# A two-block float32 transformer on one core: seven stretches of work put in another order, and the narrow level products done in 32x32 blocks

## What is computed

```python
def first_block(x, ...):
    hn = rms_norm(h, mix_norm_pre)
    rq, rk, rv, rg, aq, ak, av, iq, ik, iw = split_columns(hn @ w_in)
    ret_out = retention(rope(rq), rope(rk), rv, rg)
    att_out = dsa_attention(rope(aq), rope(ak), av, rope(iq), rope(ik), iw)
    mixed = concatenate([ret_out, att_out]) @ w_out
    h = h + rms_norm(mixed, mix_norm_post)          # post(0)
    ffn = conv_ffn(rms_norm(h, ffn_norm_pre))
    h = h + rms_norm(ffn, ffn_norm_post)            # post(1)

def hgrn2_mixer(h, ...):       # one gated linear attention, 8 heads of 128
    q, f, i, g = split(h @ w_in)
    log_f = log_sigmoid(f); k = -expm1(log_f)
    # causal: o_t = sum_s<=t (q_t * exp(G_t - G_s) . k_s) v_s, G the running sum of log_f
    o = rms_norm(o, out_norm) * silu(g)
    return o @ w_out                                # "mix2"

def nsa_mixer(h, ...):
    # keys and values of 31 compressed blocks of 32 tokens:
    kc = rms_norm(silu((k_cmp + pos) @ w1) @ w2); vc = silu((v_cmp + pos) @ w1) @ w2
    # attention over compressed keys, over all allowed keys, over a window
    return (g0 * o_cmp + g1 * o_sel + g2 * o_win) @ w_out
```

## Time and profile before

| | us |
|---|---|
| median of 3 runs | 2195.03 |
| lowest, highest | 2194.46, 2196.22 |
| profiled execution, its own time | 2194.65 |
| its span | 2192.9 |
| TensorE busy | 2090.3 (95% of the span) |
| VectorE busy | 1260.3 |
| ScalarE busy | 797.7 |
| GpSimd busy | 79.6 |

### The profile page before, as it was taken

The page is one execution under the profiler, slowest core; times in us unless marked ns, Lnnn a source line. Parts: engine busy times, 40 slices in busy tenths (PEclk is TensorE's granted clock), DMA queues, the critical chain, the costliest instruction groups (busy, mean ns, idle before and its releaser), DMA issues.

```text
span 2192.9 us, 28478 instructions
## 1 busy us (share of the span) xinstructions
PE 2090.3 (95%) x10920; PEld 1706.6 (78%) x10920; DVE 1260.3 (57%) x2218; ACT 797.7 (36%) x1444; POOL 79.6 (4%) x79
## 2 busy tenths in 40 slices
PE   6999889999998999989999999999789999999998
PEld 5778568888886878887888888779756677888887
DVE  3577747787744447654555555676676747322334
ACT  3323543333424551243322232433446634222222
POOL 0012000000000001000000000001001100000000
PEclk9999889999999999999999999999899999999999
DMA  5221025565532221102556445322300013433221
GB/s 194 88 94 39 13 75 173 176 196 168 168 128 86 87 96 59 58 20 87 173 173 201 165 163 183 125 68 90 118 1 2 2 59 123 128 98 99 100 96 48
DMA packets 146690, 231.34 MB, mean 105 GB/s; under 512 B 7324, under 2 KB 83708, under 8 KB 146556
## 3 DMA queue, kind: packets, MB, share of 16 engines
q1 hardware_dynamic: 144300, 224.05, 31.4%
q0 software_dynamic: 864, 3.15, 0.4%
q10 hardware_dynamic: 1392, 2.33, 0.3%
HBM read 227.41 MB, written 2.10 MB: 105 GB/s over the span
## 4 chain that ended last, share of the span: by engine, by line
PE 83%; DVE 9%; ACT 4%; issue 3%; DMA 0%; POOL 0%; DVEq 0%; POOLq 0%; SPq 0%; ACTq 0%
PE ps L2253 11%; PE ps L2255 11%; PE ps L2254 11%; PE ps L2280 4%; PE ps L2483 4%; PE ps L2282 4%; PE ps L2281 4%; PE ps L2211 4%; PE ps L2212 4%; PE ps L2213 4%; PE ps L2551 4%; PE ps L2481 3%; PE ps L2301 2%; PE ps L2313 2%; PE ps L2326 2%
## 5 line engine op out<-in xcount | busy, mean ns | idle before, releaser
L1557 DVE TENSOR_TENSOR w_lo<-ring,w_hi 128x1024 fp32r<-128x1024 f32 (+4 forms) x362 | 378.9, 1048 | 740.5 <-ACT w_hi L977 740.1
L977 ACT ACTIVATE w_hi<-ring 128x1024 fp32r<-128x1024 f32 (+4 forms) x362 | 329.5, 912 | 1013.0 <-PE ps L2255 469.9
L2253 PE MATMUL ps<-x_hi,w_hi 128*128 128x512 f32 x1056 | 416.2, 394 | 0.0
L2255 PE MATMUL ps<-x_hi,w_lo 128*128 128x512 f32 x1056 | 411.2, 389 | 0.0
L2254 PE MATMUL ps<-x_lo,w_hi 128*128 128x512 f32 x1056 | 410.9, 389 | 0.0
L2254 PEld LDWEIGHTS ps<-x_lo,w_hi 128*128 128x128 f32 x1056 | 198.5, 188 | 42.6 <-issue 1.9
L2253 PEld LDWEIGHTS ps<-x_hi,w_hi 128*128 128x128 f32 x1056 | 198.5, 188 | 42.4 <-issue 1.9
L2255 PEld LDWEIGHTS ps<-x_hi,w_lo 128*128 128x128 f32 x1056 | 198.3, 188 | 41.6
L2280 PE MATMUL ps<-w_hi,x_hi 128*128 128x512 f32 x480 | 187.5, 391 | 4.0 <-DVE x_hi L1633 4.0
L2282 PE MATMUL ps<-w_hi,x_hi 128*128 128x512 f32 x480 | 186.8, 389 | 0.0
L2281 PE MATMUL ps<-w_lo,x_hi 128*128 128x512 f32 x480 | 186.8, 389 | 0.0
(11 more groups left out here) (343 smaller groups left out, 3069.2 us busy)
## 6 DMA issues: line engine op xcount, KB each, us to landing
ring<-in_ada_w SPq DMA_DIRECT2D x48, 1024.0 KB, 5.1
ring<-in_ffn_w_in SPq DMA_DIRECT2D x88, 512.0 KB, 4.7
ring<-in_w_up SPq DMA_DIRECT2D x44, 512.0 KB, 4.7
ring<-in_ffn_w_out SPq DMA_DIRECT2D x20, 1024.0 KB, 4.9
ring<-in_hgrn_w_in SPq DMA_DIRECT2D x16, 1024.0 KB, 5.2
ring<-in_w_in SPq DMA_DIRECT2D x12, 1024.0 KB, 5.1
ring<-in_w_down SPq DMA_DIRECT2D x10, 1024.0 KB, 4.9
ring<-in_kv_ada_w SPq DMA_DIRECT2D x8, 1024.0 KB, 5.1
```

The source lines that it names most:

```text
L977: a.activation(to[:, n % depth, 0:src.shape[-1]], src, ACT.Copy).then_inc(s["hi_done"], 1)
L1557: v.tensor_tensor(to[:, n % depth, 0:width], src, hi[:, n % depth, 0:width].bitcast(F32), ALU.subtract).then_inc(s["lo_done"], 1)
L2253: mm(bs[j], wh[:, k, c], x_hi[:, 2 * q + k], start=first, stop=False)
L2255: ins = mm(bs[j], wl[:, k, c], x_hi[:, 2 * q + k], start=False, stop=last)
```

## The change

It has nine edits.

1. The banks of the first projection unit are shifted by one: row tile t is written to bank (t + 1) % 4, its turned form too.
2. In the DSA attention, TensorE turns the first four column tiles of mix1 (`turn_half`) ahead of the last four transposes of the attention's output, and ScalarE splits the first weight piece of mix1 after the last copy of the attention.
3. In `post(0)` ScalarE squares y of all token tiles before it squares the new x of the tiles 1 to 3, and VectorE does y_weighted and y_added of each tile together, x_normed of tile 0 after tile 1, and the other x_normed after all y_added.
4. In `post(1)` the same, with `ada_columns(0)` ahead of two x_normed in place of one.
5. The level products for the levels -1 to 4 multiply 16 blocks of 32 x 32 on the diagonal for each of the two heads, in place of 4 blocks of 128 x 128.
6. In mix2 ScalarE and VectorE split the first weight piece one loop step earlier, and TensorE multiplies the first two pieces before the turn of the last head.
7. VectorE's `split_q` (the split of x for the queries) begins at the fourth piece of the key/value projection, not at the first.
8. In PREP the fourth part of the first compression product comes before query chunk 2, the second product before chunk 3, the turn of the keys after chunk 4; VectorE's `cmp_sums`, `cmp_keys` and `cmp_turned` come one chunk earlier, ScalarE's root too.
9. In the NSA attention, the same as 2 for mix3.

```diff
--- before.py
+++ after.py
@@ -392,12 +392,12 @@
             for t in range(NT):
-                plan_bank((name, t), 4 * (k % 2) + t)
+                plan_bank((name, t), 4 * (k % 2) + ((t + 1) % NT if k == 0 else t))
             if k == 0:
...
                 for t in range(NT):
-                    plan_bank((P1_ORDER[k - 1], "T", t), 4 * ((k - 1) % 2) + t)
+                    plan_bank((P1_ORDER[k - 1], "T", t), 4 * ((k - 1) % 2) + ((t + 1) % NT if k == 1 else t))
             if k == INDEX_UNIT:
@@ -479,8 +479,8 @@
-        PREP = [("cmp1", 0, 0), ("q", 0), ("cmp1", 0, 1), ("q", 1), ("cmp1", 1, 0), ("q", 2), ("cmp1", 1, 1), ("q", 3), ("cmp2",),
-                ("q", 4), ("q", 5), ("cmpT",), ("q", 6), ("q", 7)]
+        PREP = [("cmp1", 0, 0), ("q", 0), ("cmp1", 0, 1), ("q", 1), ("cmp1", 1, 0), ("cmp1", 1, 1), ("q", 2), ("cmp2",), ("q", 3),
+                ("q", 4), ("cmpT",), ("q", 5), ("q", 6), ("q", 7)]
         for t in range(NT):
@@ -907,11 +907,12 @@
                             y_square(stage, t, half)
-                        if t:
-                            x_rms(i, t - 1)
+                        if t == 1:
+                            x_rms(i, 0)
+                    for t in range(1, NT):
+                        x_rms(i, t)
                     if i not in (2, 4):
                         early_highs(i, slice(0, 1))
-                    x_rms(i, NT - 1)
                 else:
@@ -983,6 +984,8 @@
                     else:
+                        if (n, i) == (0, 0):
+                            filled(act, ("dsa", "B", NT - 1))
                         out_weight(name, i)
@@ -1225,9 +1228,9 @@
                     a.activation(x_hi[:, i - 3], p, ACT.Copy).then_inc(s["out_hi"], 1)
-                if i > HH:
-                    out_weight("mix2", i - HH - 1)
-            for i in range(2, 8):
+                if i >= HH:
+                    out_weight("mix2", i - HH)
+            for i in range(3, 8):
                 out_weight("mix2", i)
...
@@ -1402,15 +1405,14 @@
                         y_weighted(stage, half, t)
-                    if t >= 1:
-                        y_added(stage, t - 1)
-                    if t >= 2:
-                        x_normed(i, t - 2)
-                y_added(stage, NT - 1)
-                x_normed(i, NT - 2)
+                    y_added(stage, t)
+                    if t == 1:
+                        x_normed(i, 0)
+                x_normed(i, 1)
                 if stage == 1:
                     ada_columns(0)
-                x_normed(i, NT - 1)
+                for t in range(2, NT):
+                    x_normed(i, t)
                 if i != 2:
...
@@ -2017,8 +2019,8 @@
                 low((key, k), n_piece(w, key, k), w2_lo, w2_hi)
-                if g < KT:
-                    split_q(g)
+                if 3 <= g < KT + 3:
+                    split_q(g - 3)
                 if g >= N_LAG:
@@ -2093,11 +2095,11 @@
                 q_chunk(i)
+                if i == 3:
+                    cmp_sums()
                 if i == 4:
-                    cmp_sums()
+                    cmp_keys()
                 if i == 5:
-                    cmp_keys()
-                if i == 6:
                     cmp_turned()
@@ -2291,7 +2293,7 @@
-            def attention(name, ready):
+            def attention(name, turn_half):
                 unit_of, n_units, (L, PB, PT, OT), base = ATT[name]
@@ -2329,6 +2331,8 @@
                         g = (j - 7) // 4
+                        if g == n_units // 8 - 1:
+                            turn_half()
                         b = open_bank((name, "B", g))
@@ -2337,22 +2341,26 @@
                 wait()
-                for kt in range(KT):
+                for kt in range(4, KT):
                     turn(lambda t: src[:, t, kt * P:(kt + 1) * P], (name, "T", kt))
...
-            def piece_gemm(name):
+            def gemm_piece(name, u, q, bs):
+                if u == 0:
+                    for kt in (2 * q, 2 * q + 1):
+                        evacuated(pe, (name, "T", kt))
+                split_piece((name, u), q, [(name, u, t) for t in range(NT)], bs, 512)
+            def piece_gemm(name, done=0, bs=None):
...
                 for u in range(2):
-                    bs = [None] * NT
-                    keys = [(name, u, t) for t in range(NT)]
-                    for q in range(4 if u == 0 else 2):
-                        if u == 0:
-                            for kt in (2 * q, 2 * q + 1):
-                                evacuated(pe, (name, "T", kt))
-                        split_piece((name, u), q, keys, bs, 512)
+                    if u or not done:
+                        bs = [None] * NT
+                    for q in range(0 if u else done, 2 if u else 4):
+                        gemm_piece(name, u, q, bs)
                     if u == 1:
-                        split_piece((name, u), None, keys, bs, 512, order=LAST_ORDER)
+                        split_piece((name, u), None, [(name, u, t) for t in range(NT)], bs, 512, order=LAST_ORDER)
@@ -2424,10 +2432,15 @@
                         ins.then_inc(full(("ret_o", t)), 1)
-            attention("dsa", None)
+            def turn_ret():
+                pe.wait_ge(s["mixed_ready"], NT)
+                for kt in range(4):
+                    turn(lambda t: mixed[:, t, kt * P:(kt + 1) * P], ("mix1", "T", kt))
+            attention("dsa", turn_ret)
...
             def wait_mix1():
-                pe.wait_ge(s["mixed_ready"], NT)
                 for g in range(NT):
@@ -2458,9 +2471,9 @@
                 for j in range(2):
-                    for t in range(NT):
-                        c = slice(t * P, (t + 1) * P)
-                        ins = mm(ps[:, 4 + 2 * (g % 2) + j, c], HK[:, 2 * g + j, c], HQ[:, 2 * g + j, c], start=True, stop=True)
+                    for at in range(0, S, 32):
+                        r, c = at % P, slice(at, at + 32)
+                        ins = mm(ps[r:r + 32, 4 + 2 * (g % 2) + j, c], HK[:, 2 * g + j, c], HQ[:, 2 * g + j, c], start=True, stop=True)
                 ins.then_inc(full(("lev", lv, g)), 1)
@@ -2523,9 +2536,13 @@
                         evacuated(pe, ("lev", LEVELS - 1, 3))
+                    if i == HH + 2:
+                        mix2_banks = [None] * NT
+                        for q in range(2):
+                            gemm_piece("mix2", 0, q, mix2_banks)
                     evacuated(pe, ("ho", i - 3))
                     turn(lambda t: v_tok[:, t, (i - 3) * P:(i - 2) * P], ("mix2", "T", i - 3))
-            piece_gemm("mix2")
+            piece_gemm("mix2", 2, mix2_banks)
             norm(3)
@@ -2645,7 +2662,13 @@
                     ins.then_inc(full(("cO", i - 2)), 1)
-            attention("nsa", None)
+            def turn_nsa():
+                pe.wait_ge(s["nsa_added"], len(NSA_GROUPS) - 2)
+                for kt in range(4):
+                    turn(lambda t: nsa_tok[:, t, kt * P:(kt + 1) * P], ("mix3", "T", kt))
+            attention("nsa", turn_nsa)
             out_gemm("mix3", nsa_tok, lambda: pe.wait_ge(s["nsa_added"], len(NSA_GROUPS)))
```

More of the change, by code:

```diff
@@ L1285, in _ @@
                             .then_inc(free(("nT", i, b)), 1)
-                if what == ("q", 4):
+                if what == ("q", 3):
                     act.wait_ge(s["cmp_sq"], 1)
```

## The result

| | before | after |
|---|---|---|
| median, us | 2195.48 (4 runs) | 2157.57 (4 runs) |
| lowest, highest | 2194.46, 2196.22 | 2152.64, 2158.86 |
| profiled execution: time, span | 2194.65, 2192.9 | 2157.28, 2155.5 |
| TensorE busy | 2090.3 | 2065.9 |
| mean granted clock | 0.977 | 0.982 |

The ratio is 0.9824, 95% interval 0.9806 to 0.9841. The forecast was 2168.4, so the change brought 37.4 us in the profiled executions where 26.6 were forecast. The median lies at the low end of the range (2157 to 2181); by the ratio, 0.9824 x 2195.03 = 2156.4, the time is just under it. The direction was right. Where the other 10.8 us come from is seen when the two traces are laid beside each other by stages: the time from the first product of a stage to the first product of the next.

The account below looks back on a forecast made before the run. TensorE, busy 95% of the span, was taken as the bound, so time falls only by less work or fewer waits there. Terms summed to -26.6 us; 2194.65 - 26.6 + 0.4 = 2168.4 us, range 2157 to 2181.

Parts of the forecast that it names:

- 1, first unit: First projection unit: with banks shifted, products start near 19.5 instead of 25.73, the last six at about 25.7; -6.2 us.
- 2 and 9, turns: Ends of both attentions: half the turning matmuls fill the 0.79 us wait for ScalarE's division; -0.8 and -0.7 us.
- 3 and 4, norms: Norms after first mixer and first FFN: squaring all y's first lets the last turns start earlier; -5.1 and -5.6 us.
- 5, level products: 24 level-product groups: 32 x 32 blocks cost 1.38 us a group against 1.80, at 16.4 ns a record; -10.2 us.
- Rival B: Level products: four array places overlap as two do, saving more, -38 in all, so 2156.6 us; chance 0.07.
- Rival A: Level products: narrow products cost in proportion to their records, 1.70 us a group, so 2176.6 us; chance 0.10.
- D: Level products: TensorE's instructions don't arrive fast enough, 24 cycles cost +53, so 2231 us; chance 0.04.
- E: Level products: places 32 rows apart overlap less than 64 apart, 1.83 us a group, so 2179.0 us; chance 0.08.
- 6, mix2: Second mixer: last turn behind piece 1 delays piece 2 by 3.2 us, then nine products at lower clock, 1.8; +5.0 us.
- 7, queries' splits: Key/value projection: starting x's second splitting later removes the 3.25 us wait and the low-clock products behind it; -4.6 us.
- 8, compression: Compression stage, ended by VectorE: its waits become 6.2 us for 4.6, so the last addition comes later; +1.6 us.
- The sign that I named: Query chunks of the compression stage: TensorE's waits behind VectorE's additions would be 1 to 2 us longer.

Follow-up runs that it names:

- experiment 11: Changed kernel with the first unit's bank shift and the later queries' splits both undone: 2165.44 us, ratio 0.9863 to the kernel before.
- experiment 9: Changed kernel with all eight turns of mix1 and mix3 put back behind the attention's last transposes: 2158.52 us, ratio 0.9829 to the kernel before.
- experiment 10: Changed kernel with the new order of the norms after the first mixer and first FFN undone: 2168.03 us, ratio 0.9875 to the kernel before.
- experiments 2 to 4: Changed kernel with level products ordered one array place after another (2185.62 us), two places at a time (2164.77), or in 64 x 64 blocks (2165.91).
- experiment 6: Changed kernel with mix2's new order undone, all turns ahead of its products again: 2149.95 us, ratio 0.9789 to the kernel before.
- experiment 12: Changed kernel with both mix2's new order and the compression's new order undone: 2147.25 us, ratio 0.9778 to the kernel before.

## Why the prediction was off in one term

- **1, first unit (-6.2).** Right: start at 19.80, second stop at 25.91. The level of the clock was better than reckoned (0.23 us between products from the second on), the first load later. By stages, experiment 11 has 6.9.
- **2 and 9, turns (-1.5).** Of the right sign; the sum left out that with half of the turns gone from behind the last wait the first product comes sooner, also because VectorE's low part no longer ends a wait there. With the clock full on both sides the end of the NSA attention is 1.6 shorter by its rows and 2.11 by its stage, where 0.7 was forecast. Against the kernel before there comes the lower clock on its 32 turns, 5.21 for 3.71. For the DSA attention the 1.86 of experiment 9 is no larger than the spread of that stretch between kernels with the same instructions (1.7).
- **3 and 4, norms (-10.7).** Right in mechanism and nearly in size: 13.2 by stages, 10.5 by experiment 10. The last turns of `post(0)` stand in the row that starts at 311.85, as forecast for about 313:

```profile
310.99 0.66 PE L2194 MATMUL ps<-small,arena 128*128 128x128 f32 x4 [4.18 <-DVE arena L1332]
311.85 1.98 PE L2194 MATMUL ps<-small,arena 128*128 128x128 f32 x8 [0.20 <-DVE arena L1332]
```

- **5, level products (-10.2).** This is the step that failed. I divided the 0.53 us of the sixth level's group by its 32 records, got 16.4 ns (it is 16.6), and multiplied by 64. But those 32 records lay on two places and the new 64 lie on four; in both groups 16 follow one another at a place, and only that counts. The cost is 0.92 and not 1.38, 20.7 us saved and not 10.2. Rival B had it (0.85 a group, 22 saved), at a chance of 0.07. I set it low because no row shows matmuls 8 ns apart; yet the earlier trace rows had the pair that tells: 16 records at one place 61 ns apart for 64 columns, and 32 at two places 16.4 ns apart for 32 columns. Halving the columns explains only a factor of 2, the other has to be the second place. The Trainium skill says so too (TensorEngine Tiling (Array Packing), "Key Properties": tiles can work in parallel, and a change of the mode drains the engine, which may be a part of the fixed time of a group; no run here separates it); its floor of 25 ns I had set against a mean over two places, where it is no contradiction. Rival A, a cost by records, fell with experiments 2 to 4, and D, a limit by the pace of instructions, with the changed kernel's cycle: 152 records and weight loads in 3.66 us, 42 a us, where 22.6 was the densest stretch before. (E's time leaves out the 0.4 of the sum; it should read 2179.3.)
- **6, mix2 (+5.0).** Right by mechanism, place and size: a stall of 3.05 (3.2 worked out), and eight slow products (nine worked out). Undone, it gives 5.75 in its own stage and 7.6 in the median (experiment 6).
- **7, queries' splits (-4.6).** Right: the wait fell from 3.25 to 0.27, and the projection is 3.9 shorter.

```profile
1402.01 0.50 PE L2566 MATMUL ps<-xkv_hi,w_hi 128*128 128x512 f32 x1 [0.27 <-DVE w_lo L1559]
```

- **8, compression (+1.6).** Right in mechanism and size: VectorE waits 5.38 and 0.98 in place of 1.81, 1.81 and 0.98, and experiment 12 has 1.74. The sign that I named did not come, though: TensorE's own waits behind VectorE in the query chunks grew by 0.5 us, not by 1 to 2.

```profile
1533.25 0.76 DVE L2080 TENSOR_TENSOR arena<-arena,stat 128x256 f32<-128x256 f32 x2 [5.38 <-PE ps L2624]
...
1535.59 0.41 DVE L2040 COPY small<-ps 31x256 f32<-31x256 f32 x1 [0.98 <-PE ps L2603]
```

- **What was in no step: the clock in a norm and in the compression (+2.1 and +1.3).** In the norm before the key/value projection sixteen turns ran at full clock before and in part at the lower clock after, and stages with the same instructions differ by it. The same sixteen turns, before and then after:

```profile
1423.14 1.91 PE L2184 MATMUL ps<-small,arena 128*128 128x128 f32 x16
```

```profile
1388.08 3.17 PE L2186 MATMUL ps<-small,arena 128*128 128x128 f32 x16
```

The stage from the second FFN to the key/value projection is 2.1 to 2.2 longer than before in the nine profiled kernels that have edit 6 whole, 1.4 to 1.9 in the three that lack it or have it cut to one piece, and 0.1 longer with edit 5 alone. So edit 6 can account for 0.2 to 0.8 of it at most; what brings the larger part, and by what chain, is not shown. In the compression stage one product of 32 records took 4.99 us before and 6.23 after, at a mean granted clock of 0.72 and 0.56, and VectorE's wait behind it grew from 2.57 to 3.85:

```profile
1525.23 0.76 DVE L2080 TENSOR_TENSOR arena<-arena,stat 128x256 f32<-128x256 f32 x2 [3.85 <-PE ps L2624]
```

## What to carry to other kernels

Count narrow matmuls by the place in the array, not by the instruction: the time of a group is a fixed part and the longest row at one place, so turn the places round robin. Narrowing only the operand that passes, while the weights stay 32 wide, gains nothing (28 ns for 16 columns, 25 for 32). Before moving an engine's work behind another's, look what else stands in that engine's order behind the thing that it will wait for. And a change that shifts stages changes which of them meet the lower clock, which is worth some 2 us here in either direction and belongs in the range.

## What the runs showed of the hardware that I had not expected

- 64 records of 32 columns on four places by turns: 0.76 us; on two at a time 1.11; on one 1.91. 128 records of 16 columns on one: 3.93.
- 16 records of a single column on weights of 128 columns took 1.84 us, about 106 ns each: a product of one column is not a short one when its weights are wide.
- 32 turning matmuls of the NSA attention took 3.71 us at a granted clock of 1.00, and 5.21 in the kernel before, in a stretch whose clock was lower (0.51 in its first 3 us). A row of durations from such a stretch can't be taken as the price of the same work elsewhere.
- The same norm with the same instructions got a mean clock of 0.81 in the kernel before and of 0.66 in the changed one (again the third number from the end), though nothing in it was edited:

```profile
1418.00:1427.00 9.00, 7.17 (x45) 6.08 (x46) 6.29 (x18) 5.75 (x14) 0.68 (x1) 0.81 0.16 58
```

```profile
1383.00:1393.00 10.00, 7.77 (x40) 6.72 (x40) 5.61 (x17) 5.23 (x11) 0.68 (x1) 0.66 0.18 52
```
